# Unread bf16 products in three waits of TensorE, and a separate wait for each half of the latent weights, in a two-layer streaming encoder step

## What is computed

```python
# layer 0: even_mixer (HGRN2 heads and forgetting attention); layer 1: odd_mixer (latent attention)
y = mixer(x)
x = layer_norm(ALPHA * x + y, ln_mix_g[l], ln_mix_b[l])
scores = sigmoid(x @ router_w)              # 16 experts in 4 groups
# best group, then the best two experts in it; weights w normalised
f = sum over the two experts e of ((silu(x @ w_gate[e]) * (x @ w_up[e])) @ w_down[e]) * w[e]
x = layer_norm(ALPHA * x + f, ln_ffn_g[l], ln_ffn_b[l])
...
# odd_mixer begins with
z = x @ mla_w_in                            # 1024 x 832: 512 query latents, 256 key-value latents, 64 rotary
cq, ckv, kpe = split(z)
cq, ckv, kpe = rms_norm(cq, ...), rms_norm(ckv, ...), rope(kpe, pos)
```

## Time and profile before

| | |
|---|---|
| median of three runs | 1276.92 us (1275.6 to 1278.25) |
| the profiled execution, its time | 1280.19 us |
| its span in the trace | 1277.3 us |
| mean granted clock of PE | 0.953 of full speed |
| PE busy | 1125.8 us, 88% of the span |
| DVE, ACT, POOL busy | 45%, 21%, 17% |
| mean traffic to and from memory | 168 GB/s |

### The profile page before, as it was taken

The page is one execution under the profiler, slowest core; times in us unless marked ns, Lnnn a source line. Parts: engine busy times, 40 slices in busy tenths (PEclk is TensorE's granted clock), DMA queues, the critical chain, the costliest instruction groups (busy, mean ns, idle before and its releaser), DMA issues.

```text
span 1277.3 us, 18058 instructions
## 1 busy us (share of the span) xinstructions
PE 1125.8 (88%) x6973; PEld 632.0 (49%) x6973; DVE 570.7 (45%) x1260; ACT 266.7 (21%) x634; POOL 223.3 (17%) x382
## 2 busy tenths in 40 slices
PE   8999999999899849999749899999999975999965
PEld 4557777655654523333225446676575452333322
DVE  2079878610734435634265230450253344464226
ACT  1214334321410101111002212332331010111012
POOL 0106444321101201001052300000000211100114
PEclk9999999999999959999959999999999986999987
DMA  8113211261842468999492312000104256899935
GB/s 353 67 49 132 84 66 67 82 226 58 67 176 90 152 248 313 384 421 352 164 312 77 132 48 66 1 1 1 67 1 198 82 203 245 305 396 408 328 102 199
DMA packets 41826, 214.77 MB, mean 168 GB/s; under 512 B 4488, under 2 KB 6088, under 8 KB 32400
## 3 DMA queue, kind: packets, MB, share of 16 engines
q1 hardware_dynamic: 24288, 152.57, 30.6%
q0 software_dynamic: 17168, 60.27, 15.4%
q10 hardware_dynamic: 288, 0.80, 0.2%
HBM read 180.31 MB, written 33.29 MB: 167 GB/s over the span
## 4 chain that ended last, share of the span: by engine, by line
PE 77%; DVE 9%; issue 5%; DMA 5%; ACT 3%; SPq 1%; POOL 0%; DVEq 0%; ACTq 0%; POOLq 0%
PE pair L1448 12%; PE pair L1098 9%; PE pair L1352 9%; PE pair L1469 6%; PE pair L1215 5%; PE pair L1109 5%; PE pair L1281 5%; PE pair L1545 4%; PE pair L1318 3%; PE pair L1597 2%; PE pair L1086 2%; DMA arena<-x_rows,ints 2%; PE pair L1434 2%; PE pair L1139 2%; DMA ring<-in_even_w_in 2%
## 5 line engine op out<-in xcount | busy, mean ns | idle before, releaser
L1448 PE MATMUL pair<-ring,arena 128*32 128x512 f32 x608 | 128.5, 595 | 0.0
L1098 PE MATMUL pair<-ring,xT 128*128 128x512 f32 x256 | 111.3, 593 | 0.9 <-DMA ring<-in_even_w_in 0.9
L1448 PE MATMUL pair<-arena 128*32 128x512 f32 x736 | 104.8, 626 | 8.3 <-issue 4.8
L1215 PE MATMUL pair<-xT,ring 128*128 128x296 f32 x320 | 85.1, 421 | 7.0 <-ACT arena L1644 3.0
L850 POOL TENSOR_SCALAR small<-small 128x1 f32<-128x1 f32 (+3 forms) x45 | 16.9, 375 | 410.2 <-DVE small L2160 354.2
L872 POOL TENSOR_TENSOR arena<-arena 128x128 f32<-128x128 f32 x140 | 57.3, 444 | 154.2 <-PE pair L1141 86.5
L1281 PE MATMUL pair<-arena 128*128 128x264 f32 (+5 forms) x280 | 76.5, 402 | 3.3 <-ACT arena L1634 1.8
L1098 PEld LDWEIGHTS pair<-ring,xT 128*128 128x128 f32 x256 | 48.1, 190 | 59.8 <-issue 57.9
L2086 DVE TENSOR_REDUCE small<-pair 128x1 f32<-128x144 f32 (+4 forms) x40 | 22.4, 560 | 120.3 <-PE pair L1286 120.2
L1215 PEld LDWEIGHTS pair<-xT,ring 128*128 128x128 f32 x320 | 60.4, 193 | 25.8 <-issue 9.4
L998 POOL DMA_INDIRECT arena<-x_rows,ints x26 | 26.4, 1015 | 264.5 <-PE pair L1434 161.0
(11 more groups left out here) (366 smaller groups left out, 2022.6 us busy)
## 6 DMA issues: line engine op xcount, KB each, us to landing
arena<-in_moe_w_gate_up SPq DMA_DIRECT2D x14, 2048.0 KB
ring<-in_moe_w_gate_up SPq DMA_DIRECT2D x12, 2048.0 KB, 9.8
arena<-in_moe_w_down SPq DMA_DIRECT2D x14, 1024.0 KB
y_rows<-arena SPq DMA_DIRECT2D x26, 512.0 KB, 8.3
ring<-in_moe_w_down SPq DMA_DIRECT2D x12, 1024.0 KB, 9.5
xT<-in_moe_w_gate_up SPq DMA_DIRECT2D x6, 2048.0 KB
ring<-in_even_w_in SPq DMA_DIRECT2D x5, 2048.0 KB, 8.0
y_rows<-xr POOLq DMA_DIRECT2D x12, 512.0 KB, 8.5
```

The costliest lines, as they stand in the source:

```text
L1098: last = pe.matmul(ps[0:P, 0:n], xT[:, k, 128 * i:128 * i + P], w[:, k, :], start=(k == 0), stop=(k == chunks - 1))
L1215: last = pe.matmul(ps[0:w.shape[2], 512 * s:512 * s + n], w[:, k, :], xT[:, k, n * s:n * s + n], start=(k == 0), stop=(k == KD - 1))
L1448: last = pe.matmul(bank[c, :], xgT[:, e % 2, k, c], expert_place(x)[0][:, k, :], start=(k == 0), stop=(k == KD - 1))
```

## The change

```diff
                 router_logits(l, 1)
 
+                for i in (NT - 2, NT - 1):
+                    pe.wait_ge(*ps_free[("wo", l, i)])
+                keep_busy(30)
                 pe.wait_ge(*mk_sb[l])
                 ps = claim(pe, ("rk", l))
...
                 last.then_inc(pe_full.sem(("rk", l)), 1)
+                keep_busy(4)
 
                 slot_tokens(l, 0)
                 slot_tokens(l, 1)
                 pe.wait_ge(*ps_free[("rk", l)])
                 pe.wait_ge(*ps_free[("lg", l, 1)])
                 pe.wait_ge(*ps_free[("T", 2 * l, 4)])
+                keep_busy(14)
                 experts(l)
+
+            def keep_busy(n):
+
+                for _ in range(n):
+                    pe.matmul(psum[1][:, 0:512], identb[:, :], const("lev")[:, 0:512], start=True, stop=True)
...
-            wq, wkv = weights(pe, "mi0"), weights(pe, "mi1")
-
...
+            pe.wait_ge(*cb_sb[(0, "first")])
+            keep_busy(24)
             pe.wait_ge(*r_sb[(1, 0)])
             transpose_tile(1, 0, rb[:, 0, :])
             for i in range(NT):
                 P = TILES[i]
                 pe.wait_ge(*evac[("T", 1, i)])
                 ps = claim(pe, ("mi", i))
-                for w, lo, n in ((wq, 0, 512), (wkv, 512, 320)):
+                for name, lo, n in (("mi0", 0, 512), ("mi1", 512, 320)):
+                    w = weights(pe, name)
                     for k in range(KD):
```

## The result

In 20 runs beside 20 of the kernel before, the change took 1272.76 us (median; 1266.99 to 1280.01) and the kernel before 1280.68 (1273.54 to 1286.46). The ratio is 0.9943, with a 95% interval from 0.9927 to 0.9959: 7.3 us faster, 5.3 to 9.3. The forecast was 0.9908 (11.7 us) and 1265.2 us, with a range up to 1271.5. So the sign was right and the size too large. Of the 7.6 us between forecast and median, 3.8 are the level of the runs of before, which were 1276.92 in the table ahead and 1280.68 here; the rest is the size.

What follows compares the result with a forecast made beforehand. PE, busy in 88% of the span, was taken as the bound, losing time to waits and half clock. Router stages 4.0 us plus latents 7.7 made 11.7; 1276.9 - 11.7 = 1265.2 us, range 1261 to 1271.5.

Steps and rivals of the forecast that it cites:

- What a product costs: Each unread 512-column bf16 product on PE, back to back: 0.215 us at 2.4 GHz, 0.43 at 1.2.
- The 30 and the 4 products: Router stages: 30 take 9.0 us within the 9.41 us mask wait, 4 fit the 1.58 us one-hot wait; both cost nothing.
- The 14 products: Ahead of the gathered rows in each layer: they make the transposes 1.2 us late, between 0 and 2.25.
- the swing rival: Router stages: clock falls at the slots, leaving about 0.4 us gain per layer; total 8.5 us, 1268.4 us; chance 0.20.
- The latents, 7.7 us: Start of latents: transposes start 3.9 us earlier, run 0.85 us shorter, first products 2.9 us shorter; sum 7.7 us.
- the first 512 columns take 6.87 for 9.79: Start of latents: the first 512-column products run at full clock, saving 2.9 us.
- It is kept through the experts if their weight loads move too: Experts' stage: the router stages' 4.0 us gain survives, since weight loads start when PE's products end.
- the rival with the weights: Experts' stage: starting earlier, it waits longer for weights; only 7.7 us gained, 1269.2 us; chance 0.12.
- The slower rival: Whole kernel: the change makes it slower; chance 0.06. The prediction says no more of it.
- The range: Whole kernel: 1261 to 1271.5 us, meant to leave out 2 in 10 at most.

Runs made afterwards that it cites:

- e6: The change with more unread products filling gaps in router stages and latents, plus three groups in each layer's experts' waits: 1264.8 us, 0.9884 of the kernel before.
- e2: The change without the 48 products of each router stage, leaving the split latent-weight waits and the 24 products: 0.9938 of the kernel before, 7.9 us faster.
- e5: The change plus three groups of unread products in idle waits of each layer's experts: 1268.0 us, 0.9912 of the kernel before.
- e7: The change without the 14 products ahead of the gathered rows: 0.9929 of the kernel before.
- e8: The changed kernel run and profiled once more, unaltered: 1274.0 us, 0.9956 of the kernel before.
- e11: The change without the 14 products, with three groups of unread products in each layer's experts' waits: 0.9945 of the kernel before.
- e4: The change with more unread products in the remaining gaps of router stages and latents (6, 5, 16, 3, 27 and 4): 0.9908 of the kernel before, 11.8 us faster.
- e9: The change with gaps filled in router stages, latents and experts, plus products in five waits behind the latents: 1260.5 us, 0.9861 of the kernel before.
- e12: The change with 27 products for the 24 and 4 more between the latents' first transposes and first product: 0.9952 of the kernel before.
- e1: The change without the 24 products, both latent weights awaited ahead of the first transposes; router products kept: 0.9968 of the kernel before, 4.1 us faster.
- e3: Only the split of the waits for the latent weights, no added products: 0.9976 of the kernel before, 3.1 us faster.
- e10: Only the 24 products, both latent weights awaited behind them, no router-stage products: 1.0012 of the kernel before.

## Why the prediction was wrong in size

*What a product costs:* right. In e6, 16 of them take 3.61 us in a row; less the 0.38 of one record, that is 0.215 us each.

*The 30 and the 4 products:* right. They cost nothing in any profile; PE still waits 0.6 to 1.8 us for the mask behind the 30. In the changed kernel they took 7.5 us and not 9.0, since the clock was back about 2 us behind their start and not 5.1.

*The 14 products:* nearly right. The transposes started 1.35 us behind 466.00 in layer 0, for 1.2. R was won by 1.8 us in each layer, 3.6 for 4.0. The clock fell between the groups for the slots and came back during the 14, as the swing rival had it, but back in time for the gate-up product.

*The latents, 7.7 us:* mis-sized by 2 us, at the sentence "the first 512 columns take 6.87 for 9.79". They took 8.83 in the change. I had counted 0.15 us of idle time ahead of the row tile, by a clock that comes back after 5.1 us; it came back 3.0 us behind the start of the 24, which so ended early and left 0.88. The 1.10 us for ACT's copy was in my time of 661.5 us for the end of these products, but I did not ask what it does to the clock. e2 shows that the term can come out at 7.6. With the 24 alone the clock held in three kernels, where the idle time ahead of the row tile was at most 0.54 us (e2, e5, e7), and fell in three profiles, where it was 0.67 to 1.08 (the change, e8, e11); in all four kernels with 27 and 4 it held (e4, e6, e9, e12). That the idle time decides fits this and is not shown.

*"It is kept through the experts if their weight loads move too":* this is the step that failed most. In the changed kernel the weight loads did move, and the longest waits of the gate-up products were 2.35 and 2.13 us for 2.50 and 2.35, so my reason held and the rival with the weights was wrong there (in e1 one wait grew to 3.37). But I asked only whether the weights come in time, and put at nothing what the stage's waits do to the clock once they fall at another moment. The stage was 1.8 and 1.9 us longer, 1.7 of it in each layer by one fall more. In the profiles with the 14 products (16 in e4) and the experts' waits unfilled, there were 10 falls in 10 such stages, two of them without any (the change, e1, e4, e8, e12); without any products in the router stage 2 falls in 8 (before, e2, e3, e10); with the waits filled none in 8 (e5, e6, e9, e11). Most falls cost 1.7 us, the long one of e8 more. That filling the waits takes the loss away is shown. Why the new timing meets a fall more often is so in part: six of the 10 stood behind the wait for the fourth block's rows, and none of the 2, nor the one of e7. That wait was 2.2 us on the average with the 14 (1.22 to 3.49) and 1.5 without (1.02 to 2.01), and the falls there went with waits of 2.08 us and more. Why the rows do not move with PE by the whole gain, and whether the longer wait or its moment decides, stays open.

*The swing rival* had the nearer total, 8.5 us, through a partly different place: the swing did not spoil the router's stage but the ones behind it. The Trainium skill, TensorE: Matmul & The Clock Gate, section A second HAM failure mode, says that short idle times between groups make the clock swing and that each fall and return costs throughput. The trace agrees at 654.6 in the changed kernel, behind idle times of 0.88 and 1.10 us; at 579.5 the clock fell behind a single wait of 2.35 us.

*The slower rival* was wrong: unread bf16 products raise the clock. The 24 began at 644.76, and from 647.8 on the clock was full.

*The range* left out that the three runs of before could lie off the level of more runs: the median of all 20 is 3.8 us higher. Counted from 1276.92, a gain of 7.3 us would end at 1269.6, inside the range. So half of the 7.6 us is this level, and luck; the other half is the mis-sized gain.

## What to carry to other kernels

Products that only hold the clock must reach to the moment at which the work starts: 24 of them that ended 5.7 us early were worth nothing, and with a gap of 0.9 and one of 1.1 us close together the clock fell again and part of the rest was lost. Whoever moves a stage should list the idle waits in everything behind it (the falls in the experts stood behind waits of 2.08 to 3.49 us, though other waits of up to 2.77 us passed without one), look whether they have grown, and fill them as well; the stage that is edited then shows its gain in the total. Compare stages by their lengths in the trace, because one fall is as large as the term that is looked for, and take more than one profile of each where the term is under 2 us.

## What the runs showed of the chip that was not expected

Adding work can pay twice and also cost out of sight: taking the 14 products away made two stages 2 us longer each and the whole kernel some 4 us faster than the change beside it. The same code kept the full clock over the two waits of the latents in e2, e5 and e7, and lost it in both profiles of the change and in e11; the first of the two waits was a few tenths of a us shorter where it was kept. Two of the three falls in the experts came at the same blocks in both profiles of the change.
